# Gates of the recurrent heads spread over the partitions by one rounded-format pass instead of plain fp32 passes

## The reference, cut to what matters

```
bcum = jnp.cumsum(ft, axis=-1)
dmat = bcum[..., :, None] - bcum[..., None, :] + it[..., None, :]
dmat = jnp.where(lower, dmat, -jnp.inf)
inter = bcum + m[..., None]
m_t = jnp.maximum(inter, jnp.max(dmat, axis=-1))
w_intra = jnp.exp(dmat - m_t[..., None])
s_qk = jnp.einsum('bhld,bhsd->bhls', qt, kt) * w_intra
num = ... + jnp.einsum('bhls,bhse->bhle', s_qk, vt)
h_out = num / jnp.maximum(jnp.abs(den), jnp.exp(-m_t))[..., None]
```

## Time and profile before

| | us |
|---|---|
| median of 3 runs | 3609.68 |
| lowest and highest run | 3608.98, 3610.53 |
| the profiled execution | 3608.59 |
| its span, first to last instruction | 3607.3 |
| TensorE busy in it | 3493.9 (97%) |
| VectorE, ScalarE, GpSimd busy | 1446.4 (40%), 1367.8 (38%), 1347.8 (37%) |
| mean granted TensorE clock | 0.987 of full speed |

### The profile page before, as it was taken

How to read it: one execution, slowest core, us unless ns; L and a number is a source line. 1 busy time by engine, 2 the same in 40 slices (tenths; PEclk the granted TensorE clock), 3 DMA queues, 4 the chain that set the end, 5 groups by cost and what they waited for, 6 DMA issues and landing times.

```text
span 3607.3 us, 39211 instructions
## 1 busy us (share of the span) xinstructions
PE 3493.9 (97%) x14412; PEld 2590.3 (72%) x14412; DVE 1446.4 (40%) x2764; ACT 1367.8 (38%) x2605; POOL 1347.8 (37%) x1052
## 2 busy tenths in 40 slices
PE   8999999999999999999999989989899999889999
PEld 5556777787787755677678778766588887568887
DVE  3433456534324343245654442446522123642212
ACT  2343334533223234333453322345533235643322
POOL 1222333344544322233334444433045444325444
PEclk9999999999999999999999999999999999999999
DMA  4121112223333211112122322221033332113323
GB/s 161 53 68 53 62 59 71 62 95 115 105 96 96 72 53 47 56 59 64 63 71 94 114 95 94 94 74 47 21 102 111 94 100 79 36 44 105 99 97 103
DMA packets 154751, 286.80 MB, mean 80 GB/s; under 512 B 17980, under 2 KB 20061, under 8 KB 154432
## 3 DMA queue, kind: packets, MB, share of 16 engines
q1 hardware_dynamic: 153232, 281.90, 24.6%
q10 hardware_dynamic: 1328, 2.39, 0.2%
HBM read 278.85 MB, written 5.37 MB: 79 GB/s over the span
## 4 chain that ended last, share of the span: by engine, by line
PE 85%; DVE 8%; ACT 3%; issue 2%; POOL 2%; DMA 0%; ACTq 0%; POOLq 0%; DVEq 0%
PE bank L543 23%; PE bank L545 22%; PE bank L544 22%; PE bank L601 4%; DVE work L1438 2%; POOL wl L2012 2%; PE bank L742 2%; PE bank L660 2%; PE bank L610 1%; DVE work L1389 1%; PE bank L575 1%; ACT wh L980 1%; PE bank L777 1%; PE bank L791 1%; PE bank L789 1%
## 5 line engine op out<-in xcount | busy, mean ns | idle before, releaser
L2012 POOL TENSOR_TENSOR wl<-raw,wh 128x512 fp32r<-128x512 f32 x1012 | 1316.9, 1314 | 2244.4 <-ACT wh L980 1988.4
L543 PE MATMUL bank<-Uh,wh 128*128 128x512 f32 x2720 | 1142.0, 420 | 35.1 <-POOL wl L2012 18.8
L545 PE MATMUL bank<-Uh,wl 128*128 128x512 f32 x2720 | 1068.0, 393 | 0.0
L544 PE MATMUL bank<-Ul,wh 128*128 128x512 f32 x2720 | 1066.1, 392 | 0.0
L980 ACT ACTIVATE wh<-raw 128x512 fp32r<-128x512 f32 x1012 | 602.9, 621 | 646.4 <-PE bank L545 624.2
L543 PEld LDWEIGHTS bank<-Uh,wh 128*128 128x128 f32 x2720 | 514.4, 189 | 256.8 <-issue 122.4
L544 PEld LDWEIGHTS bank<-Ul,wh 128*128 128x128 f32 x2720 | 515.6, 190 | 119.6 <-issue 20.4
L545 PEld LDWEIGHTS bank<-Uh,wl 128*128 128x128 f32 x2720 | 514.0, 189 | 112.1
L1389 DVE TENSOR_TENSOR work<-bank,rs 128x512 f32<-128x512 f32 x308 | 212.7, 691 | 886.3 <-PE bank L545 848.9
L543 PE MATMUL bank<-Hh,wh 128*128 128x512 f32 x1258 | 505.8, 402 | 6.0 <-DVE small L1602 1.9
L545 PE MATMUL bank<-Hh,wl 128*128 128x512 f32 x1258 | 490.4, 390 | 0.0
(11 more groups left out here) (209 smaller groups left out, 2850.0 us busy)
## 6 DMA issues: line engine op xcount, KB each, us to landing
raw<-in_units SPq DMA_DIRECT2D x1012, 256.0 KB, 2.9
work<-in_dft SPq DMA_DIRECT2D x6, 512.0 KB, 9.5
xT<-in_xT SPq DMA_DIRECT2D x8, 256.0 KB, 9.4
scratch<-work SPq DMA_DIRECT2D x1, 2048.0 KB, 7.7
out<-xT SPq DMA_DIRECT2D x8, 256.0 KB, 3.0
table<-scratch SPq DMA_DIRECT2D x4, 448.0 KB, 5.1
work<-in_dft SPq DMA_DIRECT2D x2, 640.0 KB, 11.4
scratch<-table SPq DMA_DIRECT2D x1, 1152.0 KB, 5.4
```

The costliest lines, as they stand in the source:

```text
L543: nc.tensor.matmul(out, H, xh, start=k == 0, stop=False)
L544: nc.tensor.matmul(out, H, xl, start=False, stop=False)
L545: mm = nc.tensor.matmul(out, L, xh, start=False, stop=k == x.kt - 1)
L2012: nc.gpsimd.tensor_tensor(g.wl[:, a:a + PK * P], g.raw[:, a:a + PK * P], g.wh[:, a:a + PK * P].bitcast(F32), ALU.subtract).then_inc(g.s_lo, 1)
```

## The change

The spreading matmuls become rounded-format matmuls with 128 rows instead of 64. Rows 0 to 63 of the moving tile hold the high part of the gates, rows 64 to 127 the low part, and the selection matrix has the same 64 rows twice, so that a single pass gives high plus low.

- The selection matrix gets a tile of its own (`select`, fp32r, 128 rows by 1024). It is loaded by two DMAs of 64 rows each into a free part of `merged`, and ScalarE copies it once in layer 0 (new step behind p == 1 of the Fourier part). The constants behind it are loaded by a third DMA and move up in their tile.
- Behind the attention loop ScalarE gets two new steps in each layer: the high parts of `gm` and `ge`, 64 rows by 512, into tile 3 of `Hh` and of `Hl`.
- Behind them VectorE gets two new steps (`gates_low`): the low parts, into rows 64 to 127 of the same tiles.
- TensorE waits for these low parts where it waited for `gm` and `ge` themselves.

```diff
@@ TensorE, recurrent heads
-        pe.wait_ge(g.landed["select"], 16)
+        pe.wait_ge(s_act, at("C", "select"))
...
-                sel = c("select", HQ)[:, (2 * h + d) * P:(2 * h + d + 1) * P]
-                pe.wait_ge(s_dve, at("V", "gm", i))
+                sel = g.select[:, (2 * h + d) * P:(2 * h + d + 1) * P]
+                pe.wait_ge(s_dve, at("V", "gml", i))
                 take(NUM[d], s_dve, "V", "nmb", i, h, d)
-                nc.tensor.matmul(bank[NUM[d]][:, :], sel, w(25)[0:HQ, :], start=True, stop=True).then_inc(
+                nc.tensor.matmul(bank[NUM[d]][:, :], sel, tile(g.Hh, 3), start=True, stop=True).then_inc(
                     s_pe, T("nmb", i, h, d))
-                pe.wait_ge(s_act, at("C", "ge", i))
+                pe.wait_ge(s_dve, at("V", "gel", i))
                 take(DEN[d], s_dve, "V", "emb", i, h, d)
-                nc.tensor.matmul(bank[DEN[d]][:, :], sel, w(26)[0:HQ, :], start=True, stop=True).then_inc(
+                nc.tensor.matmul(bank[DEN[d]][:, :], sel, tile(g.Hl, 3), start=True, stop=True).then_inc(
                     s_pe, T("emb", i, h, d))
@@ ScalarE
+            if p == 1 and i == 0:
+                act.wait_ge(g.landed["select"], 48)
+                nc.scalar.activation(g.select[:, :], g.merged[:, 6 * S:6 * S + 8 * P], ACT.Copy).then_inc(
+                    s_act, C("select"))
...
+        act.wait_ge(s_used, g.product(i, "branch0", KD - 1).done)
+        act.wait_ge(s_dve, at("V", "gm", i))
+        nc.scalar.activation(tile(g.Hh, 3)[0:HQ, :], gm, ACT.Copy).then_inc(s_act, C("gmh", i))
+        nc.scalar.activation(tile(g.Hl, 3)[0:HQ, :], ge, ACT.Copy).then_inc(s_act, C("geh", i))
         beat(i, "M", 0)
@@ VectorE
+    def gates_low(i):
+
+        gm, ge = g.gate_tiles()[6:8]
+        for name, raw, both in (("gm", gm, tile(g.Hh, 3)), ("ge", ge, tile(g.Hl, 3))):
+            dve.wait_ge(s_act, at("C", name + "h", i))
+            nc.vector.tensor_tensor(both[HQ:P, :], raw, both[0:HQ, :].bitcast(F32), ALU.subtract).then_inc(
+                s_dve, V(name + "l", i))
...
+        gates_low(i)
         beat(i, "M", 0)
@@ first loads
-    nc.scalar.dma_start(g.const[:, sel:eps], A["const"][:, sel:eps]).then_inc(landed["select"], 16)
+    for rows in (slice(0, HQ), slice(HQ, P)):
+        nc.scalar.dma_start(m[rows, 6 * S:6 * S + n], A["const"][0:HQ, sel:sel + n]).then_inc(landed["select"], 16)
+    nc.scalar.dma_start(g.const[:, sel:eps - n], A["const"][:, sel + n:eps]).then_inc(landed["select"], 16)
```

More of the change, by code:

```diff
@@ L274, in __init__ @@
         self.merged = sb("merged", KD * S)
-        self.const = sb("const", NCONST)
+        self.const, self.select = sb("const", NCONST - 8 * P), sb("select", 8 * P, F32R)
         self.table = sb("table", 7 * S)
@@ L310, in c @@
         a, n = CONST[name]
+        a -= 8 * P if a > CONST["select"][0] else 0
         return self.const[part:part + rows, a:a + n]
@@ L1654, in lambda_whole @@
     def lambda_whole(i):
-        li = CONST["lam_init"][0] + i
-        rest = CONST["lam_rest"][0] + i
         dve.wait_ge(s_act, at("C", "lam", i))
@@ L1660, in lambda_whole @@
         settle()
-        nc.vector.tensor_tensor(small[:, 45:46], small[:, 45:46], g.const[:, li:li + 1], ALU.subtract).then_inc(
+        nc.vector.tensor_tensor(small[:, 45:46], small[:, 45:46], c("lam_init")[:, i:i + 1], ALU.subtract).then_inc(
             s_dve, V())
-        nc.vector.tensor_tensor(small[:, 47:48], g.v1(i, "diff"), g.const[:, rest:rest + 1], ALU.mult).then_inc(
+        nc.vector.tensor_tensor(small[:, 47:48], g.v1(i, "diff"), c("lam_rest")[:, i:i + 1], ALU.mult).then_inc(
             s_dve, V())
@@ L1825, in layer1 @@
         if i == 0:
-            dve.wait_ge(g.landed["select"], 16)
+            dve.wait_ge(g.landed["select"], 48)
         straight(i, chains["k"])
@@ L2146, in first_loads @@
     nc.scalar.dma_start(g.const[:, 0:sel], A["const"][:, 0:sel]).then_inc(landed["const"], 16)
-    nc.scalar.dma_start(g.const[:, eps:NCONST], A["const"][:, eps:NCONST]).then_inc(landed["const"], 16)
+    nc.scalar.dma_start(g.const[:, eps - n:NCONST - n], A["const"][:, eps:NCONST]).then_inc(landed["const"], 16)
     nc.scalar.dma_start(m[0:NB, 3 * S:3 * S + L2], A["onehot2"]).then_inc(landed["spread2"], 16)
     nc.scalar.dma_start(m[0:NB, 4 * S:4 * S + 6 * P], A["rb2"]).then_inc(landed["spread2"], 16)
-    nc.scalar.dma_start(g.const[:, sel:eps], A["const"][:, sel:eps]).then_inc(landed["select"], 16)
+    for rows in (slice(0, HQ), slice(HQ, P)):
+        nc.scalar.dma_start(m[rows, 6 * S:6 * S + n], A["const"][0:HQ, sel:sel + n]).then_inc(landed["select"], 16)
+    nc.scalar.dma_start(g.const[:, sel:eps - n], A["const"][:, sel + n:eps]).then_inc(landed["select"], 16)
     extras_of(g, nc.scalar, 0)
```

## The result

The changed kernel takes 3580.95 us, the median of 4 runs (3578.80 to 3586.49), beside 3609.33 us for the kernel before (4 runs, 3607.12 to 3610.53). The two medians are 28.4 us apart. The ratio, estimated from all runs and not from the medians alone, is 0.9932, 95% interval 0.9919 to 0.9945: that is 24.5 us less, 19.9 to 29.2. A second set of 4 runs gave a median of 3585.53 us, 22.0 us less than the kernel before beside it, and a ratio of 0.9942 (0.9928 to 0.9957), 15.5 to 26.0 us less.

A forecast was written before the change was run, and what follows sets the result against it. TensorE, holding 85% of the chain of waits, was taken as the bound. Per layer 0.1 - 1.7 + 2.8 + 5.2 + 2.3 = 8.7 us, for two 17.4 us, giving 3592.3 us, range 3584 to 3599.

The forecast's parts named there:

- head 0 with its low stretch: Head 0: late new steps leave 0.1 us gain; a 3.4 us low-clock stretch behind TensorE's wait costs 1.7 us a layer.
- head 1: Head 1: nothing waits, so the shorter spreading matmuls gain 2.8 us a layer.
- head 2: Head 2: the 2.92 us wait for ScalarE stays; a shorter low-clock stretch behind it gains 5.2 us a layer.
- head 3: Head 3: the 0.64 us wait stays and the third pass waits for ScalarE; gain 2.3 us a layer.
- The pace: Spreading matmuls on TensorE: 0.23 us each in the rounded format in place of 0.89 us, one record each.
- Rival D: Spreading matmuls still run as two records of 0.43 us or more: 8.2 us slower, 3617.9 us; chance 0.03.
- my own table: Head 2's gain by low-stretch length: none 7.1 us, 3.4 us 6.0 us, 6.8 us 4.4 us, 10.2 us 2.8 us.
- the other edits: Select copy, added DMA issues, VectorE's moved copy of the turned values, and weights: taken as nothing.
- the unseen: Anywhere in the kernel: what the prediction doesn't see, near no change; chance 0.07.
- the far end of C: Low stretches of 10.2 us at both heads 0 and 2: 5.8 us less, 3603.9 us; part of a 0.2 chance.
- Rival B: No low-clock stretch at head 0 or head 2: 24.6 us less, 3585.1 us; chance 0.2.
- Rival C: Low clock stays long at heads 0 and 2, 6.8 or 10.2 us: 3597.3 or 3603.9 us; chance 0.2.

The follow-up runs named there:

- e1: The changed kernel with ScalarE making the two high parts ahead of the two weight splits instead of behind them: 3581.44 us, ratio 0.9929; again 3579.11 us, 0.9924.
- e4: The changed kernel with rounded passes over 64 rows holding the high parts alone, low parts not made: 3586.60 us, ratio 0.9947 to the kernel before.
- e3: The changed kernel with the spreading matmuls reading the same 128-row tiles as plain fp32: 3607.26 us, ratio 0.9999 to the kernel before.
- e8: e1 with the spreading matmuls reading the same 128-row tiles as plain fp32: 3600.30 us, ratio 0.9982 to the kernel before.
- e2: The changed kernel with all its new steps, but the old fp32 64-row spreading matmuls waiting for the gates alone: 3607.53 us, ratio 1.0000 to the kernel before.
- e9: The kernel before with all six product blocks ahead of the spreading passes at heads 1 to 3, nothing of the change: 3591.47 us, ratio 0.9954.
- e7: e1 with all six product blocks ahead of the spreading passes at heads 1 to 3: 3561.05 us, ratio 0.9877; again 3564.91 us, 0.9887.

## Why the prediction was right, and where it was off

Of the terms of the sum, each measured as the difference of the two profiles' distances to the same head:

| term, a layer | forecast | layer 0 | layer 1 |
|---|---|---|---|
| head 0 with its low stretch | -1.6 | -1.4 | -1.4 |
| head 1 | 2.8 | 2.8 | 2.8 |
| head 2 | 5.2 | 5.5 | 5.5 |
| head 3 | 2.3 | 2.2 | 2.2 |
| sum | 8.7 | 9.1 | 9.1 |

(For instance head 2: 504.20 - 445.31 = 58.89 us from head 2 to head 3 before, 495.60 - 442.17 = 53.43 us after, 5.5 us less.)

- **The pace.** Right: 0.23 us a pass at head 1, but for the first step of 0.31 us, and one record each. Rival D, that the passes keep the old price, fell with it.
- **Head 0.** Right in every step but for a few tenths of a microsecond (without the clock the gain was 0.3 us, forecast 0.1): ScalarE's high parts behind the second split, VectorE's low part held to 0.55 us behind GpSimd's end, a wait of 2.30 us against 2.3, a low stretch of 3.4 us in both layers. e1 shows that the place in ScalarE's queue causes the wait, and e4 divides it; no run takes out GpSimd's hold alone. That the wait causes the low stretch is right for the change against e1, but e4 shows that a wait of 0.86 us with 64-row passes has one too.
- **Head 2.** The mechanism was right and the size a little low: the stretch was 3.4 us, for which my own table said 6.0 us, and I took 5.2 between that and the next case. Measured 5.5. The table's 6.0 us put the start of the low stretch at the end of the wait, where a part of it is lost in the third pass's wait for ScalarE anyway. It started 1.2 to 1.3 us later (443.5 against 442.17 in layer 0, and 441.0 against 439.84 in the second profile), so nearly all of it fell on work: 7.1 - 1.7 = 5.4 us. The reason that I gave for the fall in length was half of it: I put it down to the rounded passes coming sooner. By e3 and e8 the 128 rows alone bring it to 3.4 us, in fp32 as well, where the clock rose before any rounded product had run; by e4 the format does so over 64 rows too.
- **Heads 1 and 3, and the other edits.** Right within 0.1 us; e2 shows no cost of the other edits. The select copy took 1.04 us in ScalarE's hole.
- **The absolute time.** The sum missed by 4.7 us in the profiled execution (22.1 against 17.4): 0.8 us in the heads, 1.7 us ahead of 187 us, 0.4 us between the two layers' heads, and 1.8 us behind them. The second and the last are mainly low stretches, near the start and at 1742, that came or went with nothing near them changed, so they are luck and no part of the change. The median of the first set lies 5.5 us lower still. Its runs tell the same: span 3577.5 us at a mean granted clock of 0.991, against 3585.2 us at 0.989 for the profiled one, and 0.002 of the span is 7.2 us. The clock is given to 0.001, which is 3.6 us, so the two agree, and no more than that. Why the changed kernel spreads by 7.7 us over four runs where the kernel before spread by 3.4 us is open; in a later set the kernel before spread by 7.4 us over 19 runs. So the range was too narrow for the clock: I had let each stretch come or go once, and the runs of one program differ by more than that.

The chances don't add up as written: the unseen alone has 0.07, so the far end of C (3603.9 us, above the border of 3602.5) had no share in "same", though the text gives it one.

Rival B (no low stretch, 24.6 us less, 3585.1 us) was nearer to both measured medians than the forecast was, and the first set's ratio gives its 24.5 us. It has the wrong mechanism in every profile taken: all eight waits at heads 0 and 2 in the two profiles of the change were followed by a low stretch. Whether they were in the fastest runs, of which there is no profile, stays open. Rival C (long low stretches) did not occur.

## What to carry to other kernels

Price a shorter instruction at each of its places, by what TensorE waits for there once it is short: here the same edit was worth -1.4, 2.8, 5.5 and 2.2 us a layer at the four heads. A new step on a helper engine belongs ahead of whatever in that queue waits for the very engine that will wait for the step; moving two instructions up was worth 3.7 to 6.0 us a layer in the profiles, 4.3 us where the clock at head 2 was the same. And before making work shorter, look for work that can be put into the waits: six product blocks moved gave over the heads nearly as much as the whole change (e9, 8.6 against 9.1 us a layer), and with it more than either (e7).

## What the runs showed of the hardware

- fp32 passes over 64 rows behind a 2.9 us wait went with 10.2 us of low clock (1.2 GHz), four times of four (before and e2); passes over 128 rows, rounded or fp32, with 3.4 us, eight times of eight for e3, e8 and the change. The clock rose amid fp32 passes over 128 rows. e1's four waits of the same length were less regular: 3.4 us in layer 0 of both profiles, none and 6.8 us in layer 1.
- A low stretch of 3.4 us stood behind a wait of 0.86 us (e4), but behind none of the 2.04 us waits of the changed kernel's two profiles, and behind none of head 3's 0.63 us. Over all thirteen profiles, 10 of the 26 waits of 2.04 us had one. The length of the wait alone doesn't decide.
- Passes over 64 rows among work over 128 rows cost some slow steps: at head 1 of e4 the last pass and the first product take 0.33 us each, where the change, with 128 rows, has 0.23 us. With four such places a layer, e8 and the kernel before differ by 1.0 us beyond the clock.
- A VectorE subtraction of two SBUF tiles beside a GpSimd one: 0.69 us becomes 1.40 or 1.77 us, and it ends 0.55 us behind GpSimd. The Trainium skill (SBUF — State Buffer, section "Who interferes with whom") says that the one that starts second is blocked; e1 bears that out, where the subtraction that started 0.12 us ahead of GpSimd took its usual 0.69 us and GpSimd's run took 1.72 us instead of the 1.29 us of the same run in the change:

```profile
332.25 1.72 POOL L2029 TENSOR_TENSOR wl<-raw,wh 128x512 fp32r<-128x512 f32 x1 [5.25 <-ACT wh L981]
```
